# The first modulation group moves to steps 1 and 3 of the local attention, and ScalarE gets a one-column exponential behind the barrier

## The chip, the cores and the metric

The kernel is one program on 1 NeuronCore of a Trainium2 chip. The metric is device time in microseconds (us), the median of several executions. Engines are named as in the profile: PE (TensorE matmul), PEld (its weight load), DVE (VectorE), ACT (ScalarE), POOL (GpSimd), SP (SyncE, which here only issues transfers).

## What is computed

One inference step of a transformer with DEPTH = 2 layers over 640 tokens (128 of context, 512 latent: five tiles of 128), width 1024, all in float32. What matters here is that each layer has six modulation vectors per kind of token, and three groups of attention heads:

```python
def modulate(cvec, w_mod_l, b_mod_l):
    m = jnp.einsum('bd,de->be', jax.nn.silu(cvec), w_mod_l) + b_mod_l
    return jnp.split(m[:, None, :], N_MOD, axis=-1)     # sh1, sc1, g1, sh2, sc2, g2, each 1024 wide

sh1, sc1, g1, sh2, sc2, g2 = modulate(c, w_mod_l, b_mod_l)
h = rmsnorm(x, norm1_l) * (1 + sc1) + sh1
...   # projections; latent attention (A), window attention (B), 2-D neighbourhood attention (C)
x = x + g1 * (heads_out @ w_out_l)
h2 = rmsnorm(x, norm2_l) * (1 + sc2) + sh2
...   # mixture of experts on h2, added with g2
```

`w_mod` is 1024 x 6144 per layer (24 MB), so the modulation is a large read of weights for very few rows of output (one for latent, one for context tokens).

## The kernel before, in words

Each engine runs its own instruction list in program order, and the lists are tied by semaphores. A layer has four stages: entry and input projection (1), local attention, heads B and C (2), the projections of heads A (3), and their attention with the output projection (4); then the experts. All engines but SP meet at a barrier (`meet`) between stages 1, 2, 3 and 4.

The modulation of a layer is done in three groups of 2048 columns (`mod_group(L, g, ks)`): g = 0 is needed at the layer's entry, g = 1 and 2 (rows g1 to g2) later. A group is eight k slices of 128 input channels, each four matmuls of 512 columns that lie in four column strips of PE; the kernel does it in halves of four slices. Group 1 and 2 of the layer and group 0 of the next layer are done during stage 2, spread into the steps of its attention pipeline. Their weights lie in the four buffers `slot[0..3]` of `ring`, which in stage 1 hold the input projection's weights. SP (`mod_load`, line 1002) issues the load of group 1 in eight transfers of 1 MB: as soon as the last projection has left slots 0 and 1, half 0 of slots 0 and 1, then half 1 of both; once it has left slots 2 and 3, half 0 of slot 2, half 0 of slot 3, half 1 of slot 2, half 1 of slot 3. `mod_in[0]` counts half 0 of all four slots, `mod_in[1]` half 1. SP reloads half 0 with group 2 when `mod_half` tells that half 0 has been used, and half 1 when the group is finished.

Stage 2 is a software pipeline over 20 pairs of heads and tiles, in 24 steps. In step s, PE does (in this order) `turn(s-3, 0)` (transpose the normalised probabilities), `scores(s)`, `turn(s-3, 1)`, `values(s-4)` and whatever of the modulation is put there; DVE does `maximum(s)` (line 1820, both halves), `normalise(s-1)`, and for the modulation `mod_rows` (adds the bias, line 1665) and `mod_columns2`; ACT does the copies of the transposes and `exps(s)`. `scores(s)` can start once DVE's `maximum(s-1)` has released both score banks. `values` start at step 4. Where the pipeline is still filling, PE is given matmuls of zeros (`spin`, line 507) into PSUM bank 7, the bank that the modulation also uses: four each in steps 0 and 1, and three in step 3. The modulation groups stand at steps `MOD_AT = (3, 10, 17)` and the step behind each.

In ACT's list the first exponential of stage 2 is preceded by a load of its function table.

Of the kernel before, what the change touches and what calls it, by code (L numbers as in the profile page):

```python
# [29 lines left out]
ACT = mybir.ActivationFunctionType  # L30
# [5 lines left out]
DEPTH = 2  # L36
# [34 lines left out]
WHOLE = [[], [2, 4]]  # L71
ORDER = [4, 0, 1, 2, 3]
AT = [ORDER.index(t) for t in range(TILES)]
MOD_AT = (3, 10, 17)

CHUNKS = [(0, 416), (416, 384), (800, 512), (1312, 384)]
C_CQ, C_CKV, C_KPE, C_QS, C_KS, C_QN, C_KN = 0, 256, 384, 416, 672, 800, 1056
# [61 lines left out]
def program(nc, t_in, t_out):  # L139
    with ExitStack() as ctx:  # L140
        def sb(name, shape, dt=F32):
            return ctx.enter_context(nc.sbuf_tensor(name, shape, dt))
# [31 lines left out]
        cst, at = {}, 0  # L174
# [6 lines left out]
        mhalf = sb("mhalf", [P, 8])  # L181
# [149 lines left out]
        stat = {n: sb("st_" + n, [P, 8]) for n in ("mx", "m2", "nm", "sm", "es", "ri")}  # L331
# [3 lines left out]
        def two(b, n=1024):  # L335
            return ps[:, b:b + 2, :].rearrange("p a b -> p (a b)")[:, 0:n]
# [133 lines left out]
        def queries(pr, h):  # L470
            if pr["kind"] == "mla":
                return qT[0:QK, pr["heads"][h], pr["t"] * P:(pr["t"] + 1) * P]
            q = qs if pr["kind"] == "swa" else qn
            return q[64 * h:64 * h + 64, pr["c"], pr["t"] * P:(pr["t"] + 1) * P]

        def keys(pr, h, lo, hi):
            if pr["kind"] == "mla":
                return kT[0:QK, pr["heads"][h], lo:hi]
            if pr["kind"] == "swa":
                return ksT[64 * h:64 * h + 64, lo:hi]  # L480
            return knT[64 * h:64 * h + 64, pr["c"], lo:hi]

        def value_rows(pr, h, j):
            if pr["kind"] == "mla":
                return v_mla[:, j, pr["heads"][h] * 64:pr["heads"][h] * 64 + 64]
            at = 64 * h if pr["kind"] == "swa" else 128 + 64 * pr["heads"][h]
            return v_loc[:, j, at:at + 64]
# [4 lines left out]
        def split(phase, n):  # L492

            return (n, 0) if n == 1 or phase == 2 else (3, n - 3)
# [5 lines left out]
        def _(pe):  # L500
            def transpose(out, in_):
                return pe.transpose(out, in_, ident)  # L502

            def spin(b, n):

                for _ in range(n):
                    pe.matmul(ps[:, b, 0:256], zeros[:, 0:P], zeros[:, :], start=True, stop=True)
# [45 lines left out]
            def attention(L, phase):  # L553
                pairs = PAIRS[phase]
                base = PPL * L + PBASE[phase]

                def scores(p, halves):
                    pr = pairs[p]
                    for h in halves:
                        S[h].take(pe, ("s", L, phase, p))  # L560
                    for n, (at, lo, hi) in enumerate(pr["k"]):
                        for h in halves:
                            mm = pe.matmul(two(2 * h)[:, at:at + hi - lo], queries(pr, h), keys(pr, h, lo, hi),  # L563
                                           start=(at % 512 == 0), stop=True, skip_group_check=True)
                            if n == len(pr["k"]) - 1:
                                mm.then_inc(S[h].full, 1)

                def turn(p, h):
                    n = pairs[p]["n"]
                    a, d = split(phase, n)  # L570
                    T.take(pe, ("p", L, phase, p, h), frees=2 if d else 1)
                    pe.wait_ge(pn_done, base + 2 * p + h + 1)
                    for j in range(n):
                        o = two(4)[:, j * P:(j + 1) * P] if j < a else ps[:, 5, (j - a) * P:(j - a + 1) * P]
                        mm = transpose(o, pb[phase][:, p % DEEP, h, j * P:(j + 1) * P])
                    mm.then_inc(T.full, 1)

                def values(p):
                    pr = pairs[p]
                    O.take(pe, ("o", L, phase, p))  # L580
                    pe.wait_ge(T.free, T.freed[("p", L, phase, p, 1)])
                    for j in range(pr["n"]):
                        for h in range(2):
                            mm = pe.matmul(ps[64 * h:64 * h + 64, 6, 0:P], value_rows(pr, h, pr["v"][j]),  # L584
                                           pt[phase][p % 2][h][:, j * P:(j + 1) * P],
                                           start=(j == 0), stop=(j == pr["n"] - 1))
                    mm.then_inc(O.full, 1)

                for s in range(STEPS[phase]):
                    turning = 3 <= s < len(pairs) + 3  # L590
                    if phase == 4:
                        ranks(L, s - 1)
                    if phase == 2:
                        if turning:
                            turn(s - 3, 0)
                        if s == 3:
                            spin(7, 3)
                        if s < len(pairs):
                            scores(s, (0, 1))
                        if s < 2:  # L600
                            spin(7, 4)
                        if turning:
                            turn(s - 3, 1)
                        if s == len(pairs) + 1:
                            for h in range(2):
                                pe.wait_ge(S[h].free, S[h].freed[("s", L, 2, len(pairs) - 1)])
                        if s > len(pairs):
                            spin(3, 1)
                    else:
                        for h in range(2):  # L610
                            if s < len(pairs):
                                scores(s, (h,))
                                if s == 0:
                                    spin(7, 2)
                            if turning:
                                turn(s - 3, h)
                    if 4 <= s < len(pairs) + 4:
                        values(s - 4)
                    if phase == 2:
                        for g, at in enumerate(MOD_AT):  # L620
                            if s in (at, at + 1) and (g < 2 or L < DEPTH - 1):
                                ks = range(4 * (s - at), 4 * (s - at) + 4)
                                mod_group(L + g // 2, (g + 1) % 3, ks)
                        for g in (1, 2):
                            if s == MOD_AT[g - 1] + 3:
                                mod_columns2(L, g)
                        if s == MOD_AT[2] + 3 and L < DEPTH - 1:
                            mod_columns(L + 1)
                    if phase == 4:
                        if s == 1:  # L630
                            shift_logits(L)
                        beside(L, s)
# [113 lines left out]
            for L in range(DEPTH):  # L746
# [98 lines left out]


                attention(L, 4)
                E0 = NE * L

# [349 lines left out]
        def _(act):  # L1199
# [118 lines left out]
            for L in range(DEPTH):  # L1318
# [50 lines left out]
                    act.wait_ge(x7_out[TILES - 1], 16 * L)  # L1369
                meet(act, "act")  # L1370

                attention(L, 2)
                meet(act, "act")

# [283 lines left out]
        def _(dve):  # L1658
# [140 lines left out]
            def attention(L, phase):  # L1799
# [46 lines left out]
                for s in range(STEPS[phase] + 1):  # L1846
                    turning = 3 <= s < len(pairs) + 3
                    if phase == 4 and s == 2:
                        shift_logits(L)
                    if phase == 4 and s >= 1:  # L1850
                        ranked(L, s - 1)
                    for h in range(2):
                        if s < len(pairs):
                            maximum(s, h)
                        if turning and phase == 4:
                            copy(s - 3, h)
                    if phase == 4 and s >= 1:
                        projected(L, s - 1)
                    if 1 <= s <= len(pairs):
                        normalise(s - 1)  # L1860
                    if phase == 4 and s >= 1:
                        beside(L, s - 1)
                    if phase == 2:
                        for g, at in enumerate(MOD_AT):
                            if s == at + 2 and (g < 2 or L < DEPTH - 1):
                                mod_rows(L + g // 2, (g + 1) % 3)
                        for g in (1, 2):
                            if s == MOD_AT[g - 1] + 4:
                                mod_columns2(L, g)
                        if s == MOD_AT[2] + 4 and L < DEPTH - 1:  # L1870
                            mod_columns(L + 1)

            def projected(L, s):
# [140 lines left out]
            for L in range(DEPTH):  # L2014
# [19 lines left out]
                for s in range(TILES + 1):  # L2034
# [25 lines left out]
                    if s >= 1:  # L2060
                        for i in ([5, 0] if s == 1 else [s - 1]):
# [6 lines left out]
                            ks = ps[:, 5, 256:384] if i < 5 else ps[:, 5, 0:P]  # L2068
# [297 lines left out]
```

## Time and profile before

| | |
|---|---|
| median of 3 runs | 1338.06 us (1335.75 to 1340.5) |
| the profiled execution's own time | 1338.34 us |
| its span, first to last instruction | 1336.3 us |
| mean granted TensorE clock | 0.991 of full speed |
| PE busy | 1279.6 us, 96% of the span |
| DVE, ACT, POOL busy | 613.7, 358.8, 152.5 us |
| mean DMA rate | 234 GB/s |

Busy time of PE is modelled from pipelined matmuls, so 96% does not mean that it works at its peak. A stretch is read from the timeline of one engine: start, duration, and in brackets how long the engine sat idle before it and what released it. A float32 matmul stands as two records. A transfer has the time of its issue, and its landing counted from there.

### The profile page before, as it was taken

Reading aid. Unit: us, or ns where it says so; the run is one execution under the profiler, and the core shown is the slowest. Engines: PE = TensorE matmul, PEld = TensorE weight load, DVE = VectorE, ACT = ScalarE, POOL = GpSimd, SP = SyncE. Lnnn points to the kernel's source line nnn. Section 1 sums busy time; section 2 is a strip of 40 time slices with the busy share of each in tenths; the row PEclk is TensorE's granted clock in tenths of the full one; section 3 lists DMA queues with packets and bytes.
Section 4 is the critical chain, followed back from the end, with each engine's and each line's share of the span. In section 5 each row is a group of like instructions: output and inputs, shape, how many; then the busy total and the mean of one; then the engine's idle time right before and its main releaser. Section 6 shows DMA issues by size and latency. Waiting matters only on the chain. (4 is left out here: it accounts for less than half of the span.)

```text
span 1336.3 us, 17216 instructions
## 1 busy us (share of the span) xinstructions
PE 1279.6 (96%) x6042; PEld 735.3 (55%) x6042; DVE 613.7 (46%) x1519; ACT 358.8 (27%) x931; POOL 152.5 (11%) x257
## 2 busy tenths in 40 slices
PE   6999999999999999999999999989999999999997
PEld 3555555565666564444455555566666656444443
DVE  0132266444566463433343224655556536344438
ACT  1121255434343210000012114563444311100001
POOL 2210220000000110000142003000000011000014
PEclk9999999998999999999999999999899999999999
DMA  9976996499111489999694038430201139999966
GB/s 355 363 248 220 347 332 254 162 359 327 42 64 64 168 333 398 361 374 367 260 334 161 16 140 291 151 128 15 88 33 64 63 130 352 404 368 360 362 270 246
DMA packets 125441, 313.16 MB, mean 234 GB/s; under 512 B 9882, under 2 KB 58426, under 8 KB 112688
## 3 DMA queue, kind: packets, MB, share of 16 engines
q1 hardware_dynamic: 90896, 243.13, 49.8%
q0 software_dynamic: 12848, 45.39, 9.0%
q10 hardware_dynamic: 21616, 23.60, 5.3%
q8 instruction: 46, 0.75, 0.2%
q14 instruction: 35, 0.29, 0.1%
HBM read 232.14 MB, written 80.71 MB: 234 GB/s over the span
## 5 line engine op out<-in xcount | busy, mean ns | idle before, releaser
L790 PE MATMUL ps<-ring,big 128*128 128x384 f32 (+2 forms) x640 | 230.7, 520 | 1.7 <-DVE big L1773 1.3
L790 PEld LDWEIGHTS ps<-ring,big 128*128 128x128 f32 x640 | 120.3, 190 | 104.6 <-issue 63.7
L871 PE MATMUL ps<-ring,arena 128*128 128x512 f32 x384 | 169.3, 594 | 1.9 <-ACT arena L1406 1.9
L502 PEld LDWEIGHTS ps<-consts,arena 128*128 128x128 f32 (+2 forms) x880 | 103.7, 143 | 79.1 <-issue 50.9
L502 PE MATMUL ps<-consts,arena 128*128 128x128 f32 (+2 forms) x880 | 129.7, 278 | 15.7 <-ACT arena L1227 6.6
L711 PE MATMUL ps<-ring,big 128*128 128x512 f32 x320 | 143.0, 598 | 0.8
L563 PE MATMUL ps<-arena 64*128 64x128 f32 (+5 forms) x576 | 137.9, 430 | 6.1 <-DVEq L1822 3.4
L1227 ACT ACTIVATE arena<-ps 128x384 f32<-128x384 f32 (+3 forms) x140 | 69.1, 493 | 221.3 <-PE ps L502 221.3
L871 PEld LDWEIGHTS ps<-ring,arena 128*128 128x128 f32 x384 | 71.2, 190 | 83.1 <-issue 83.1
L563 PEld LDWEIGHTS ps<-arena 64*128 64x128 f32 (+1 forms) x576 | 79.4, 196 | 65.8 <-issue 57.8
L711 PEld LDWEIGHTS ps<-ring,big 128*128 128x128 f32 x320 | 59.0, 190 | 70.4 <-issue 66.4
L1410 ACT ACTIVATE arena<-ps 128x256 f32<-128x256 f32 x32 | 12.3, 385 | 300.6 <-PE ps L871 300.6
L1809 DVE TENSOR_REDUCE st_nm<-ps 128x1 f32<-128x640 f32 (+1 forms) x80 | 57.2, 717 | 75.2 <-PE ps L563 74.8
L584 PE MATMUL ps<-arena 128*64 128x128 f32 x1104 | 85.9, 280 | 1.2 <-DVEq L1963 1.2
L2122 DVE TENSOR_TENSOR arena<-arena,ps 128x256 f32<-128x256 f32 x32 | 13.5, 421 | 154.4 <-ACT arena L1410 154.4
L584 PEld LDWEIGHTS ps<-arena 128*64 128x64 f32 x1104 | 66.4, 137 | 11.9 <-issue 9.6
L2140 DVE TENSOR_TENSOR arena<-ps,arena 128x512 f32<-128x512 f32 x64 | 44.2, 691 | 55.1 <-PE ps L892 55.1
L1218 ACT ACTIVATE ring<-ps,st_nm 128x640 f32<-128x640 f32 (+1 forms) x80 | 56.4, 705 | 20.6 <-DVE st_nm L1809 20.2
L892 PE MATMUL ps<-ring,arena 128*128 128x512 f32 x128 | 57.8, 594 | 1.0 <-DVE arena L2128 1.0
L892 PE MATMUL ps<-arena 128*128 128x512 f32 x128 | 57.8, 594 | 1.0 <-DVE arena L2128 1.0
L1215 ACT ACTIVATE arena<-arena,st_nm 128x640 f32<-128x640 f32 (+4 forms) x80 | 54.0, 676 | 14.8 <-DVEq L1823 14.4
L871 PE MATMUL ps<-arena 128*128 128x512 f32 x128 | 56.3, 592 | 0.0
(237 smaller groups left out, 1481.9 us busy)
## 6 DMA issues: line engine op xcount, KB each, us to landing
ring<-in_w_mod SPq DMA_DIRECT2D x40, 1024.0 KB, 11.8
ring<-in_w_up SPq DMA_DIRECT2D x22, 1024.0 KB, 9.7
ring<-in_w_gate SPq DMA_DIRECT2D x22, 1024.0 KB, 7.6
slots<-zeros ACTq DMA_DIRECT2D x8, 2560.0 KB, 14.4
slots<-zeros SPq DMA_DIRECT2D x8, 2560.0 KB, 20.2
arena<-in_w_down SPq DMA_DIRECT2D x16, 1024.0 KB, 12.7
arena<-slots SPq DMA_DIRECT2D x30, 512.0 KB, 6.4
slots<-arena POOLq DMA_DIRECT2D x30, 512.0 KB, 9.6
```

What stands on the lines that cost most here:

```text
L502: return pe.transpose(out, in_, ident)
L563: mm = pe.matmul(two(2 * h)[:, at:at + hi - lo], queries(pr, h), keys(pr, h, lo, hi), start=(at % 512 == 0), stop=True, skip_group_check=True)
L584: mm = pe.matmul(ps[64 * h:64 * h + 64, 6, 0:P], value_rows(pr, h, pr["v"][j]), pt[phase][p % 2][h][:, j * P:(j + 1) * P], start=(j == 0), ...
L711: mm = pe.matmul(ps[:, b, :], hoT[:, i, k, :], slot[2 + half][:, k, :], start=(k == 0), stop=(k == KD - 1))
L790: mm = pe.matmul(ps[:, c, 0:CHUNKS[c][1]], hT[:, s, k, :], slot[c][:, k, 0:CHUNKS[c][1]], start=(k == 0), stop=(k == KD - 1))
L871: mm = pe.matmul(ps[:, b, :], xgT[:, b, k * P:(k + 1) * P], w_gu[q][:, :, k, :], start=(k == 0), stop=(k == KD - 1))
L892: mm = pe.matmul(ps[:, 2 + n, :], hidT[:, b, k * P:(k + 1) * P], w_dn[q][:, k, n * 512:(n + 1) * 512], start=(k == 0), stop=(k == 1))
L1215: act.activation(buf[:, 0:w], buf[:, 0:w], ACT.Exp, bias=stat["nm"][:, col], scale=-1.0, accum_out=stat["sm"][:, col]).then_inc(ex_done, 1)
L1218: act.activation(buf[:, 0:w], two(2 * h, w), ACT.Exp, bias=stat["nm"][:, col], scale=1.0, accum_out=stat["sm"][:, col]).then_inc(S[h].free, 1)
L1227: act.activation(pt[phase][p % 2][h][:, 0:a * P], two(4, a * P), ACT.Copy).then_inc(T.free, 1)
L1809: dve.tensor_reduce(nm, src, AX.X, ALU.max, negate=True).then_inc(nmax_done, 1)
L2140: return TT(yb[:, b, n * 512:(n + 1) * 512], ps[:, 2 + n, :], rowG[:, n * 512:(n + 1) * 512], ALU.mult)
```

## The change

The modulation group 1 of each layer has its half 0 at the end of step 1 and its half 1 at the end of step 3 (before: steps 3 and 4). The spins of steps 1 and 3 go; that of step 0 stays. DVE's `mod_rows` and both `mod_columns2` of this group come one step earlier. Groups 2 and 0 stay in steps 10, 11 and 17, 18. In ACT's list a one-column exponential stands between the barrier and the attention of stage 2; its result is written to a statistics buffer that stage 2 does not use.

```diff
-MOD_AT = (3, 10, 17)
+MOD_AT = ((1, 3), (10, 11), (17, 18))
...
                         if turning:
                             turn(s - 3, 0)
-                        if s == 3:
-                            spin(7, 3)
                         if s < len(pairs):
                             scores(s, (0, 1))
-                        if s < 2:
+                        if s == 0:
                             spin(7, 4)
...
                         for g, at in enumerate(MOD_AT):
-                            if s in (at, at + 1) and (g < 2 or L < DEPTH - 1):
-                                ks = range(4 * (s - at), 4 * (s - at) + 4)
+                            if s in at and (g < 2 or L < DEPTH - 1):
+                                ks = range(4 * at.index(s), 4 * at.index(s) + 4)
                                 mod_group(L + g // 2, (g + 1) % 3, ks)
                         for g in (1, 2):
-                            if s == MOD_AT[g - 1] + 3:
+                            if s == MOD_AT[g - 1][1] + 2:
                                 mod_columns2(L, g)
...
                 meet(act, "act")
+                act.activation(stat["es"][:, 0:1], mhalf[:, 0:1], ACT.Exp)
                 attention(L, 2)
...
                         for g, at in enumerate(MOD_AT):
-                            if s == at + 2 and (g < 2 or L < DEPTH - 1):
+                            if s == at[1] + 1 and (g < 2 or L < DEPTH - 1):
                                 mod_rows(L + g // 2, (g + 1) % 3)
                         for g in (1, 2):
-                            if s == MOD_AT[g - 1] + 4:
+                            if s == MOD_AT[g - 1][1] + 3:
                                 mod_columns2(L, g)
```

## Rows read from the trace of the kernel before

**Rows 1.** The page: busy time of PE.

```profile
PE 1279.6 (96%) x6042; PEld 735.3 (55%) x6042; DVE 613.7 (46%) x1519; ACT 358.8 (27%) x931; POOL 152.5 (11%) x257
```

**Rows 2.** Timeline of PE, layer 0, stage 2, steps 1 to 5.

```profile
165.05 1.99 PE L507 MATMUL ps<-zeros 128*128 128x256 f32 x8
167.16 1.14 PE L563 MATMUL ps<-arena 64*128 64x384 f32 x8
...
168.61 1.46 PE L507 MATMUL ps<-zeros 128*128 128x256 f32 x6
170.34 0.92 PE L563 MATMUL ps<-arena 64*128 64x256 f32 x8 [0.26 <-DVEq L1822]
...
172.04 3.64 PE L520 MATMUL ps<-ring,sc 128*32 128x512 f32 x32
175.61 0.66 PE L502 MATMUL ps<-consts,arena 128*128 128x128 f32 x4
...
178.44 3.64 PE L520 MATMUL ps<-ring,sc 128*32 128x512 f32 x32
182.01 0.66 PE L502 MATMUL ps<-consts,arena 128*128 128x128 f32 x4
```

**Rows 3.** Timeline of PE, layer 1, the same steps.

```profile
813.96 1.99 PE L507 MATMUL ps<-zeros 128*128 128x256 f32 x8
816.04 1.14 PE L563 MATMUL ps<-arena 64*128 64x384 f32 x8
...
820.89 3.64 PE L520 MATMUL ps<-ring,sc 128*32 128x512 f32 x32
...
830.87 0.66 PE L502 MATMUL ps<-consts,arena 128*128 128x128 f32 x4
```

**Rows 4.** Single loads of line 1002: issue duration (ns), start, then time to landing.

```profile
L1002 SPq DMA_DIRECT2D ring<-in_w_mod x1: 509/509/509, 157.1 to 157.1; - x1
...
DMA to landing us min/median/max: 12.6/12.6/12.6
...
L1002 SPq DMA_DIRECT2D ring<-in_w_mod x1: 509/509/509, 805.6 to 805.6; - x1
...
DMA to landing us min/median/max: 8.9/8.9/8.9
...
L1002 SPq DMA_DIRECT2D ring<-in_w_mod x1: 995/995/995, 806.7 to 806.7; - x1
DMA to landing us min/median/max: 15.4/15.4/15.4
```

**Rows 5.** Timeline of ACT, layer 0, the first exponentials of stage 2.

```profile
163.10 1.28 ACT L1215 ACT_TABLE_LOAD   x1 [2.59 <-DVEq L1823]
...
166.10 0.73 ACT L1215 ACTIVATE arena<-arena,st_nm 128x513 f32<-128x513 f32 x1 [0.41 <-DVEq L1823]
```

**Rows 6.** Timeline of DVE, layer 1, `maximum` of steps 4 to 6 and `mod_rows`.

```profile
826.01 0.62 DVE L1820 CUSTOM_DVE_ANT_0 arena<-ps,consts,sink 128x384 f32<-128x384 f32 x1 [1.92 <-PE ps L563]
...
832.62 0.75 DVE L1820 CUSTOM_DVE_ANT_0 arena<-ps,consts,sink 128x512 f32<-128x512 f32 x1 [3.07 <-PE ps L563]
...
835.61 0.68 DVE L1665 TENSOR_TENSOR mrow<-ps,mrow 128x512 f32<-128x512 f32 x1
836.55 0.75 DVE L1820 CUSTOM_DVE_ANT_0 arena<-ps,consts,sink 128x512 f32<-128x512 f32 x1 [0.26 <-DVE mrow L1665]
```

**Rows 7.** Stretches: length, busy time by engine, PEclk, DMA share, GB/s.

```profile
140.00:166.00 26.00, 25.34 (x103) 15.68 (x102) 7.26 (x22) 6.69 (x21) 5.98 (x14) 1.00 1.04 364
...
295.20:298.60 3.40, 3.40 (x30) 3.40 (x30) 0.65 (x4) 0.54 (x4) 0.00 (x0) 0.92 1.04 342
...
302.00:312.20 10.20, 10.20 (x27) 5.24 (x27) 3.47 (x9) 4.14 (x14) 0.00 (x0) 0.52 1.04 345
...
940.30:947.10 6.80, 6.44 (x18) 3.81 (x19) 2.62 (x11) 3.08 (x13) 0.00 (x0) 0.54 0.55 221
```

**Rows 8.** Groups of PE by line, from 294.6 to 298.5 us.

```profile
L549 PE MATMUL ps<-wr,modc 128*128 128x24 f32 x32 | 3.8, 270 | 0.0
```

**Rows 9.** Timeline of PE, start of the kernel.

```profile
9.29 3.64 PE L520 MATMUL ps<-arena,sc 128*32 128x512 f32 x16 [9.29 <-DMA arena<-in_w_mod]
12.87 3.79 PE L507 MATMUL ps<-zeros 128*128 128x256 f32 x12
16.58 1.92 PE L520 MATMUL ps<-arena,sc 128*32 128x512 f32 x16
18.43 2.86 PE L507 MATMUL ps<-zeros 128*128 128x256 f32 x12
```

More of the change, by code:

```diff
@@ L620, in attention @@
                         for g, at in enumerate(MOD_AT):
-                            if s in (at, at + 1) and (g < 2 or L < DEPTH - 1):
-                                ks = range(4 * (s - at), 4 * (s - at) + 4)
+                            if s in at and (g < 2 or L < DEPTH - 1):
+                                ks = range(4 * at.index(s), 4 * at.index(s) + 4)
                                 mod_group(L + g // 2, (g + 1) % 3, ks)
                         for g in (1, 2):
-                            if s == MOD_AT[g - 1] + 3:
+                            if s == MOD_AT[g - 1][1] + 2:
                                 mod_columns2(L, g)
-                        if s == MOD_AT[2] + 3 and L < DEPTH - 1:
+                        if s == MOD_AT[2][1] + 2 and L < DEPTH - 1:
                             mod_columns(L + 1)
@@ L1864, in attention @@
                         for g, at in enumerate(MOD_AT):
-                            if s == at + 2 and (g < 2 or L < DEPTH - 1):
+                            if s == at[1] + 1 and (g < 2 or L < DEPTH - 1):
                                 mod_rows(L + g // 2, (g + 1) % 3)
                         for g in (1, 2):
-                            if s == MOD_AT[g - 1] + 4:
+                            if s == MOD_AT[g - 1][1] + 3:
                                 mod_columns2(L, g)
-                        if s == MOD_AT[2] + 4 and L < DEPTH - 1:
+                        if s == MOD_AT[2][1] + 3 and L < DEPTH - 1:
                             mod_columns(L + 1)
```

## The prediction

> **What bounds the kernel now.** The page comes first: PE is busy 96% of the span [rows 1], so a change pays only where it shortens PE's list or a stretch in which PE waits or spins. Then I read PE's timeline in the steps that the diff touches, once for each layer [rows 2, 3]. In layer 0, step 1 ends with eight spin records at 165.05, `scores(2)` start at 167.16, `scores(3)` at 170.34, half 0 of the modulation at 172.04, step 4 at 175.61, half 1 at 178.44 and step 5 at 182.01 [rows 2]: 16.96 us from the start of the spins of step 1 to step 5. Layer 1 has the same rhythm, 813.96 to 830.87, 16.91 us [rows 3]. The reader should see two things. PE waits in front of `scores(3)` for DVE (0.26 us, behind the spin of step 3 [rows 2]): the pipeline is filling, and one score step costs 3.18 us because DVE's `maximum` must release the banks first, whatever PE does in between. And the two halves, 3.57 us each to the next instruction, stand beside spins that compute nothing. The third view is that of the loads, because the moved half needs its weights some 7 us earlier. The fourth is the granted clock.
>
> **Part by part.** *The spin of step 3* goes for nothing: it lies inside the wait for DVE [rows 2], so removing it gains 0. Its cover is DVE's `maximum(2)`, and its cost, were DVE not there, would be its 1.46 us.
>
> *The spin of step 1* is replaced by half 0. The two intervals around it are 2.11 us (165.05 to 167.16) in layer 0 and 2.08 us in layer 1. In its place stands the wait for `mod_in[0]`, if there is one, and 3.57 us.
>
> *The wait.* `mod_in[0]` is full when half 0 of slot 3 has landed. That is the second load of the later batch: issued 157.1 in layer 0 and 12.6 us on its way, so landed at 169.7; in layer 1 issued 805.6, 8.9 us, landed at 814.5 [rows 4]. PE arrives at 165.05 in layer 0 (after the last score record of step 1 is issued) and at 813.96 in layer 1. So PE waits 4.7 us in layer 0 and 0.6 us in layer 1. The difference between the layers is the DMA queues: from 140 to 166 us they are busy all the time (share 1.04, 364 GB/s [rows 7]), so the eight 1 MB loads come one behind the other. Behind the waiting instruction on PE stands `scores(2)`, and for that DVE and then ACT wait; SP's reload of half 0 comes when `mod_half` is raised, 169.7 + 3.57 = 173.3 instead of 175.6, which nothing needs before step 10.
>
> *The rest of the fill.* From `scores(2)` to `scores(3)` 3.18 us, from there to the half behind it 1.70 us, 3.57 us for it, then step 4 without a half, 175.61 to 178.44, 2.83 us [rows 2]. Step 4's own half (3.57 us) is gone. Half 1 is in time: layer 0 wants it at 178.2, and before, it ran at 178.44 with no wait; layer 1 wants it at 823.0, and its last load lands at 806.7 + 15.4 = 822.1 [rows 4].
>
> | us | layer 0 | layer 1 |
> |---|---|---|
> | wait for half 0 | 4.7 | 0.6 |
> | half 0 | 3.57 | 3.57 |
> | `scores(2)` to `scores(3)` | 3.18 | 3.15 |
> | to half 1 | 1.70 | 1.70 |
> | half 1 | 3.57 | 3.57 |
> | step 4 | 2.83 | 2.83 |
> | sum | 19.55 | 15.42 |
> | before | 16.96 | 16.91 |
> | difference | +2.6 | -1.5 |
>
> (For layer 1 the score step and the 1.70 come from the 4.85 us between 816.04 and 820.89, step 4 from the 9.98 us between 820.89 and 830.87 less two halves [rows 3].)
>
> *Does it survive step 5?* Steps 5 to 9 have no modulation and DVE is nearly full there, so DVE's own chain must be checked. Before, DVE idled 3.07 us ahead of `maximum(5)` under half 1 [rows 6]; that idle time is gone. In layer 1 `maximum(4)` starts 1.54 us into step 4 (826.01 against a step start of 820.89 + 3.58 = 824.47), so at 826.55 + 1.54 = 828.1; by the 3.93 us from `maximum(5)` to `maximum(6)` with `mod_rows` in between [rows 6], `maximum(5)` starts at 832.0 (before 832.62), and `maximum(6)`, without `mod_rows` (0.68 + 0.26), at 835.0 (before 836.55): 1.5 us gained there too. POOL's and ACT's share in this can take or give some 0.9 us per layer (the 0.6 us gain at `maximum(5)` against 1.5): I keep that as a bound.
>
> *DVE's additions* only move one step ahead; they keep their distance to the half.
>
> *The exponential.* It brings the table load (1.28 us [rows 5]) in front of the wait for the first `maximum`, in which ACT idles 2.59 us. Before, ACT had caught up by the second pair: it idled 0.41 us ahead of it, waiting for DVE [rows 5]. No instruction of PE before step 3 needs an exponential. So it gains 0; if this cover were gone, 1.28 us per layer, 2.6 in all, is the upper bound, and one small instruction of ACT in an idle stretch is the lower one, 0. The Trainium skill (ScalarE: Activation LUTs, What ACT_TABLE_LOAD costs) puts a switch at about 1.28 us plus 1.38 us of drain, 2.66 us; by that the upper bound would be 5.3 us for both layers. The trace agrees with the 1283 ns alone and shows no idle stretch of that size behind it.
>
> **The clock.** Rows show TensorE at its lower level (1.2 GHz) twice behind a warm stretch: PEclk 0.52 over 302.0 to 312.2 and 0.54 over 940.3 to 947.1 [rows 7]. What PE did before the first: 3.8 us of matmuls with 24 columns each [rows 8], busy by the record, but little streamed. After the change PE streams nothing for 4.7 us in layer 0, less than it did there. So I expect the clock to fall in or just behind that wait. The price from both sides: 0 if it holds; at the lower level the 16 records of a half-size group took 3.64 us against 1.92, and 12 spins 3.79 against 2.86, together 2.65 us more over the first 7 us of dense work [rows 9]; a low stretch as long as those of rows 7 would reach half 1 as well and cost up to 5. Half 0 alone at 1.2 GHz costs 3.6 at most, half of it if the clock returns while it runs, 1.8. I take 2.2, between 1.8 and 2.65, since the dense half follows at once. The Trainium skill (TensorE: Matmul & The Clock Gate, Why this matters for your kernels) warns of PE-idle gaps between bursts for the same reason. That the trace agrees with it in full no row shows, since no warm stretch before has so long a wait.
>
> **Sum.** +2.6 - 1.5 + 2.2 = +3.3 us on the profiled execution's 1338.34, of which the span is 1336.3 and 2.0 us lie around it. The median of the runs, 1338.06, is 0.3 lower; on it, 1341.3 us.
>
> **The rivals.**
> *A. The wait, and the clock falls* (forecast, 0.50): 1341.3, own range 1339.8 to 1344.
> *B. The wait, the clock holds* (0.27). For: every step around it is dense, and one low stretch behind a weak one is not a rule. Against: rows 7 and 8. 1338.06 + 1.1 = 1339.2.
> *C. Faster: the weights are there* (0.13). The loads land before PE arrives in both layers. Decisive is a landing of slot 3's half 0 at 166 or earlier in layer 0, 3.7 us earlier than the row. Then each layer gains 16.9 less 14.85, 2.1 us: 1338.06 - 4.2 = 1333.9; with part of it, 1336. Against: the queues are full [rows 7], and none of the earlier issues is moved.
> *D. Low for longer, or in both layers* (0.10): the spins also kept PE streaming in steps 1 and 3, and without them the clock falls in both layers or stays low over half 1: 1338.06 + 1.1 + 5 = 1344.2 and above.
>
> **Range and chances.** B, A and the lower half of D are inside, C's partial gain too: 1336.0 to 1344.8 leaves out about 0.08 below and 0.08 above; without C, A and B alone are 1338.5 to 1344. A measurement of this kernel tells about 0.3%, 4.0 us, from no change: 1334.0 and 1342.1 are the bounds. Faster: half of C, 0.06. Slower: D and some 0.4 of A, 0.30. Within: 0.64.
>
> **What would show it.** Right: in layer 0 an idle stretch of PE of 4 to 5 us ahead of line 520, released by a DMA, `scores(2)` near 173.3, and PEclk under 1 between 168 and 178; in layer 1 a wait under 1 us, `scores(2)` near 818.1 and step 5 near 1.5 us earlier relative to the start of stage 2; ACT_TABLE_LOAD right behind the barrier with `exps(1)` at its old distance to `maximum(1)`. Wrong: no DMA release ahead of line 520, or ACT ahead of its old place with PE following it, or step 10 no later in layer 0 although `scores(2)` is (then another engine paces the steps in between).

## The result and the profile after

| us | before | after |
|---|---|---|
| median | 1338.35 (1334.87 to 1342.05, 13 runs) | 1343.4 (1340.38 to 1347.93, 13 runs) |
| profiled execution, its span | 1338.34, 1336.3 | 1347.93, 1345.9 |

The ratio after to before is 1.0046, 95% interval 1.0031 to 1.0061: some 6 us slower (4 to 8); the medians lie 5.05 us apart. The profiled execution after is the slowest of its 13, so its span (+9.6) overstates the change. What can be compared to a tenth of a microsecond is the length of stage 2, from the first score matmul to the first projection matmul of stage 3. The timeline of PE gives both ends; first the kernel before:

```profile
161.21 0.49 PE L563 MATMUL ps<-arena 64*128 64x256 f32 x2 [0.23 <-PEq L424]
261.13 0.67 PE L815 MATMUL ps<-wuq,arena 128*128 128x512 f32 x1 [0.23 <-POOLq L424]
...
809.77 0.49 PE L563 MATMUL ps<-arena 64*128 64x256 f32 x2 [0.23 <-PEq L424]
902.23 0.67 PE L815 MATMUL ps<-wuq,arena 128*128 128x512 f32 x1 [0.23 <-POOLq L424]
```

and the changed kernel:

```profile
161.38 0.49 PE L563 MATMUL ps<-arena 64*128 64x256 f32 x2 [0.23 <-PEq L424]
266.99 0.67 PE L813 MATMUL ps<-wuq,arena 128*128 128x512 f32 x1 [0.39 <-POOLq L424]
...
816.33 0.49 PE L563 MATMUL ps<-arena 64*128 64x256 f32 x2 [0.23 <-PEq L424]
909.92 0.67 PE L813 MATMUL ps<-wuq,arena 128*128 128x512 f32 x1 [0.23 <-POOLq L424]
```

Stage 2 took 99.9 and 92.5 us and takes 105.6 and 93.6: +5.7 in layer 0, +1.1 in layer 1. These 6.8 us lie within the ratio's 4 to 8. The rest of the 9.6 us lies between the two stages 2 and behind the second, and varies as much among the kernels below (546 to 549 us between them, 434 to 440 behind).

The fill of layer 0, timeline of PE (answers to [rows 2]):

```profile
164.15 1.14 PE L563 MATMUL ps<-arena 64*128 64x384 f32 x8
170.08 5.64 PE L520 MATMUL ps<-ring,sc 128*32 128x512 f32 x32 [4.79 <-DMA ring<-in_w_mod]
175.65 1.14 PE L563 MATMUL ps<-arena 64*128 64x384 f32 x8
...
178.83 0.92 PE L563 MATMUL ps<-arena 64*128 64x256 f32 x8 [1.56 <-DVEq L1821]
...
180.53 3.64 PE L520 MATMUL ps<-ring,sc 128*32 128x512 f32 x32
184.10 0.65 PE L502 MATMUL ps<-consts,arena 128*128 128x128 f32 x4
...
186.94 0.66 PE L502 MATMUL ps<-consts,arena 128*128 128x128 f32 x4
```

The reader should see the wait of 4.79 us that a DMA ended, and behind it a half that takes 5.64 us instead of 3.64. The load it waited for, single, with its time to landing (answers to [rows 4]):

```profile
L1000 SPq DMA_DIRECT2D ring<-in_w_mod x1: 508/508/508, 157.2 to 157.2; - x1
...
DMA to landing us min/median/max: 12.7/12.7/12.7
```

157.2 + 12.7 = 169.9, and PE starts at 170.08. The changed kernel in layer 1 (answers to [rows 3]):

```profile
821.29 3.64 PE L520 MATMUL ps<-ring,sc 128*32 128x512 f32 x32 [0.69 <-DMA ring<-in_w_mod]
824.86 1.14 PE L563 MATMUL ps<-arena 64*128 64x384 f32 x8
...
829.89 5.13 PE L520 MATMUL ps<-ring,sc 128*32 128x512 f32 x32
834.95 0.66 PE L502 MATMUL ps<-consts,arena 128*128 128x128 f32 x4
...
837.78 0.65 PE L502 MATMUL ps<-consts,arena 128*128 128x128 f32 x4
```

Here the wait is 0.69 us, and it is half 1, in step 3, that is slow, 5.13 us. The DMA queues of the changed kernel show what differs between the layers. From 140 to 166 us all engines are busy (share 1.04), and over 140 to 170 us a second queue takes 38.6% of them:

```profile
q1 hardware_dynamic: 3405, 6.78, 60.3%
q10 hardware_dynamic: 3568, 3.62, 38.6%
```

ACT issued two fills of `slots` with zeros, 2560 KB each, at 134.1 and 134.6; the second landed 19.9 us later, 10 us after the first load of the modulation had been issued. Over 796 to 826 us, in layer 1, this queue moves nothing. That the wait of layer 0 would be as short as that of layer 1 without these fills was not tried.

Stretches of the changed kernel (length, busy time by engine, PEclk, DMA share, GB/s; answers to [rows 7]):

```profile
162.00:168.00 6.00, 3.29 (x22) 2.23 (x18) 3.37 (x10) 3.19 (x10) 6.00 (x12) 0.95 1.05 391
168.00:174.60 6.60, 4.52 (x24) 1.26 (x28) 0.56 (x2) 0.13 (x2) 0.01 (x1) 0.53 0.98 359
174.80:180.00 5.20, 3.39 (x31) 1.77 (x22) 2.62 (x8) 2.00 (x5) 0.18 (x1) 1.00 0.55 182
...
830.20:833.40 3.20, 3.20 (x20) 0.71 (x16) 2.60 (x5) 1.48 (x5) 2.19 (x2) 0.57 1.00 341
833.60:840.00 6.40, 6.21 (x59) 3.77 (x52) 2.88 (x8) 3.15 (x8) 2.81 (x4) 1.00 1.04 386
```

The granted clock averages 0.53 over 168 to 174.6 in layer 0 and 0.57 over 830.2 to 833.4 in layer 1, which is the lower level (1.2 GHz) for most of either stretch. In the kernel before it was full throughout stage 2, here over the whole of it in each layer:

```profile
161.20:261.10 99.90, 92.15 (x812) 55.88 (x812) 54.98 (x184) 54.73 (x141) 13.26 (x26) 1.00 0.69 250
809.80:902.20 92.40, 84.75 (x744) 53.67 (x744) 53.66 (x180) 54.73 (x141) 13.46 (x26) 1.00 0.50 178
```

ACT's list (answers to [rows 5]) has the table load right behind the barrier, and the second pair's exponential stands where it stood, now with 1.43 us of idle time before it instead of 0.41:

```profile
160.78 1.28 ACT L1370 ACT_TABLE_LOAD   x1
162.07 0.20 ACT L1370 ACTIVATE st_es<-mhalf 128x1 f32<-128x1 f32 x1
...
166.27 0.72 ACT L1213 ACTIVATE arena<-arena,st_nm 128x513 f32<-128x513 f32 x1 [1.43 <-DVEq L1822]
```

### The profile page after: what moved, and what is told of

Same layout as the page of the kernel before. It is cut to its first block and busy times, and to the rows that moved or that the text cites. A ratio compares the mean times of both kernels' runs of the same rounds, so it can differ in the third digit from the quotient of the medians.

```text
span 1345.9 us, 17162 instructions
## 1 busy us (share of the span) xinstructions
PE 1277.8 (95%) x6014; PEld 731.1 (54%) x6014; DVE 614.0 (46%) x1519; ACT 359.2 (27%) x933; POOL 152.0 (11%) x257
```

## The experiments

Theory W is the prediction's: the wait for the weights in layer 0 and the clock behind it make the loss. Theory S: the removed spins let the clock fall by themselves. X: the exponential has a price. All lengths are those of stage 2 in one profiled execution; ratios are against the kernel before on the same chip, with their 95% interval.

| kernel | ratio | layer 0 | layer 1 |
|---|---|---|---|
| before | | 99.9 | 92.5 |
| changed | 1.0046 (1.0031 to 1.0061) | 105.6 | 93.6 |
| e1 exponential alone | 1.0006 (0.9987 to 1.0026) | 99.9 | 92.4 |
| e2 changed, spins in both gaps | 1.0023 (1.0008 to 1.0038) | 103.4 | 91.8 |
| e3 half 0 loaded first | 1.0098 (1.0079 to 1.0117) | 107.2 | 97.9 |
| e4 steps 2 and 3 | 0.9994 (0.9982 to 1.0007) | 100.9 | 91.2 |
| e5 new place in layer 0 alone | 1.0046 (1.0028 to 1.0065) | 105.8 | 92.6 |
| e6 new place in layer 1 alone | 0.9993 (0.9976 to 1.0011) | 99.9 | 93.6 |
| e7 before without the spins | 1.0029 (1.0009 to 1.0048) | 102.6 | 96.1 |
| e8 layer 0 as before, layer 1 in 2 and 3 | 0.9997 (0.9980 to 1.0013) | 99.9 | 91.3 |
| e9 e2 with POOL's additions early | 1.0039 (1.0022 to 1.0055) | 102.7 | 93.1 |
| e10 e8 with POOL's additions early | 1.0076 (1.0053 to 1.0099) | 105.2 | 94.2 |
| e11 changed, spins in step 1 alone | 1.0019 (1.0003 to 1.0035) | 105.0 | 91.9 |
| e12 changed, spins in step 3 alone | 1.0040 (1.0023 to 1.0057) | 105.6 | 91.4 |

**e1, the exponential alone.**

```diff
                 meet(act, "act")
+                act.activation(stat["es"][:, 0:1], mhalf[:, 0:1], ACT.Exp)
                 attention(L, 2)
```

> The kernel before with the one-column exponential alone. Theory W (PE's wait for the weights of half 0 in layer 0, and the clock that falls behind it, make the loss) and theory S (the removed spins let the clock fall, wait or no wait): no difference, the table load stands earlier in ACT's list and nothing else moves, 1338.4 us. Theory X (the exponential has a price or a gain of its own): up to 2.6 us less, or as much of the 5 us loss as is its own.

1337.64 us against 1337.73. The interval alone would leave room for 2 us either way, but stage 2 is as long as before in both layers. X falls.

**e2, spins back under the wait and in step 3.**

```diff
+                        if s == 3:
+                            spin(6, 3)
                         if s < len(pairs):
                             scores(s, (0, 1))
                         if s == 0:
                             spin(7, 4)
+                        if s == 1:
+                            spin(7, 9 if L == 0 else 1)
```

> The changed kernel with spins put back where they can't cost time: nine in layer 0 and one in layer 1 in front of half 0, inside the wait for its weights, and three in step 3 into the bank of the values, which is free there. W and S both say that the clock holds through the fill: the half in layer 0 takes 3.6 us instead of 5.6, that in layer 1 3.6 instead of 5.1, so some 3.5 us less than the changed kernel, about 1340 us; the wait of 4.8 us in layer 0 stays, now under spins, so it is still 1 to 2 us slower than before. If the clock is not part of the cause, it stays at 1343.4.

1341.24 us. By the ratios half of the loss is gone, though their intervals overlap; the stages show it more sharply. Timeline of PE in layer 0 of e2:

```profile
164.73 4.15 PE L507 MATMUL ps<-zeros 128*128 128x256 f32 x18
169.53 3.64 PE L520 MATMUL ps<-ring,sc 128*32 128x512 f32 x32 [0.65 <-DMA ring<-in_w_mod]
...
184.38 0.66 PE L502 MATMUL ps<-consts,arena 128*128 128x128 f32 x4
```

The weights come no earlier, but the half takes 3.64 us again. The granted clock is 1.00 throughout stage 2, and the stage is 2.2 us shorter than in the changed kernel in layer 0 and 1.8 in layer 1: that is the clock's part. Without it, layer 0 is still 3.5 us longer than before, and layer 1 0.7 shorter (+3.49 and -0.64 by the timeline).

**e3, half 0 of all four slots first.**

```diff
                 for half in range(2):
                     sp.wait_ge(S[half].full, S[half][("in", L, TILES - 1)])
-                    for part in range(2):
-                        mod_load(L, 1, part, (2 * half, 2 * half + 1))
+                    mod_load(L, 1, 0, (2 * half, 2 * half + 1))
+                mod_load(L, 1, 1)
```

> The changed kernel with one edit on SP: half 0 of all four slots is loaded first, half 1 of all four behind it. W: half 0 of slot 3 lands at about 164.5 us in layer 0, so PE doesn't wait at half 0 and waits some 1.6 us at half 1 (landing about 175); in layer 1 neither waits by more than 0.5. Without a clock fall about 1337 us. S: the clock falls in spite of it, in one or both layers, and costs 1.5 to 2 each: 1339 to 1341.

In layer 0 PE did not wait at half 0 (it started at 164.78), as said, and yet the kernel is the slowest of all, 1% behind. Half 1 waits 5.57 us there and, with the clock low again, takes 6.58. In layer 1, where no wait over 0.5 us was expected, PE waits 0.77 us at half 0 and 3.83 at half 1. Half 1 of layer 0, timeline of PE:

```profile
178.87 6.58 PE L520 MATMUL ps<-ring,sc 128*32 128x512 f32 x32 [5.57 <-DMA ring<-in_w_mod]
```

A stretch of e3 shows why the landing came 4 us later than I had worked out:

```profile
155.00:158.00 3.00, 2.57 (x17) 1.74 (x15) 0.62 (x2) 1.62 (x6) 0.00 (x0) 1.00 0.45 130
```

With only two loads for slots 0 and 1 issued early, the queue runs dry until the last projection frees slots 2 and 3: 130 GB/s over 155 to 158, where the kernel before moved 406:

```profile
155.00:158.00 3.00, 2.82 (x17) 1.86 (x15) 0.57 (x2) 1.34 (x5) 0.00 (x0) 1.00 1.06 406
```

The early half 1 of slots 0 and 1 is what fills that gap. This order got half 0 in on time at the cost of half 1. Whether another order has both in time was not tried.

**e4, half 0 in step 2, the spins of step 1 kept.**

```diff
-MOD_AT = ((1, 3), (10, 11), (17, 18))
+MOD_AT = ((2, 3), (10, 11), (17, 18))
...
-                        if s == 0:
+                        if s < 2:
                             spin(7, 4)
```

> The changed kernel with half 0 in step 2 instead of step 1, and the spins of step 1 kept. W: in layer 0 PE reaches half 0 at 168.3, the weights land at 169.8, so it waits 1.5 us and not 4.8, and half 0 lies where PE waits for DVE anyway: step 5 some 0.6 us earlier than before in layer 0 and 2.1 us earlier in layer 1, less 0.6 each that the following steps take back; no clock fall: 1336.5 us. S: the missing spins of step 3 alone let the clock fall: 1338 to 1340.

1337.4 us, no difference from before. PE waited 1.60 us at half 0 and 0.49 at half 1 in layer 0, and there is no low clock in stage 2, although the spins of step 3 are missing in both layers. Locally it is +1.0 and -1.2 us.

**e5 and e6, one layer each.** `MOD_AT` becomes a list by layer, with the spins of the untouched layer kept:

```diff
-MOD_AT = ((1, 3), (10, 11), (17, 18))
+MOD_AT = [((1, 3), (10, 11), (17, 18)), ((3, 4), (10, 11), (17, 18))]    # e5; e6 the other way round
```

> The changed kernel with the new place of the halves in layer 0 alone; layer 1 has them in steps 3 and 4 with its spins, as before. W (the wait of layer 0 and the clock that falls behind it): the whole loss stays, 1342.5 to 1343.5 us, with stage 2 of layer 0 about 5.7 us longer than before and that of layer 1 unchanged. S (the removed spins cost in both layers): about half of the loss, 1340.5.

> The counterpart: halves in steps 1 and 3 in layer 1 alone, layer 0 as before. W: a wait of 0.7 us, stage 2 of layer 1 between 1 us shorter (clock holds) and 1.1 us longer (clock falls behind step 3 as in the changed kernel); 1337.4 to 1339.2 us, no difference that can be told. S: 1340.5.

By the ratios the whole loss is layer 0's (1.0046 against 1.0046), and layer 1 alone can't be told from before. By the stages layer 0 has 5.7 of the 6.8 us: stage 2 of layer 1 in e6 is 1.1 us longer as in the changed kernel, with a low clock again. The changed kernel's price is the place of half 0 in the layer where the loads are late.

**e7, the kernel before without the spins of steps 1 and 3.**

> The kernel before without the spins of steps 1 and 3, nothing else. They stand inside PE's waits for DVE, so without a clock effect nothing moves: 1338 us (W). S: the clock falls in the fill of stage 2 in one or both layers, and the half behind it takes 5 us or more instead of 3.6: 1339.5 to 1342.

```diff
-                        if s == 3:
-                            spin(7, 3)
...
-                        if s < 2:
+                        if s == 0:
                             spin(7, 4)
```

1343.55 us, 1.0029: here S was right and W, by which nothing moves, was wrong. Timeline of PE in layer 0 of e7, and behind it in layer 1:

```profile
167.85 1.14 PE L563 MATMUL ps<-arena 64*128 64x384 f32 x8 [2.04 <-DVEq L1820]
...
171.01 1.65 PE L563 MATMUL ps<-arena 64*128 64x256 f32 x8 [1.54 <-DVEq L1820]
...
173.42 5.58 PE L520 MATMUL ps<-ring,sc 128*32 128x512 f32 x32
...
818.98 2.02 PE L563 MATMUL ps<-arena 64*128 64x384 f32 x8 [2.01 <-DVEq L1820]
...
822.98 1.65 PE L563 MATMUL ps<-arena 64*128 64x256 f32 x8 [1.15 <-DVEq L1820]
```

and two stretches of it, one in each layer:

```profile
171.10:177.70 6.60, 6.60 (x35) 2.75 (x39) 4.37 (x10) 2.77 (x8) 2.37 (x2) 0.52 0.58 211
...
819.60:829.60 10.00, 8.86 (x46) 4.16 (x46) 6.31 (x16) 3.87 (x12) 2.55 (x3) 0.51 0.29 111
```

In layer 0 the scores start at the same distances as before, since PE waits there for DVE, and the clock falls in the second of the two gaps without spins, 2.0 and 1.5 us long: `scores(2)` still take 1.14 us, `scores(3)` 1.65 instead of 0.92. In layer 1 it falls behind the first gap already: `scores(2)` take 2.02 us. So one gap of 2.0 us was enough there. Stage 2 gets 2.7 and 3.6 us longer.

**e11 and e12, one cover each.** Which of the two gaps of the changed kernel does it?

> The changed kernel with spins in front of half 0 alone (nine in layer 0, one in layer 1), none in step 3. If the long wait is what lets the clock fall, layer 0 holds (stage 2 103.4 us) and layer 1, whose wait is only 0.7 us, is as in the changed kernel (93.6, a fall near step 3). If the gap of step 3 does it, both layers fall and cost 1.5 to 2 each.

> The changed kernel with the three spins of step 3 alone, none in the wait. If the wait is what lets the clock fall in layer 0, stage 2 stays at 105.6 us there; layer 1 holds (91.8), since only step 3 was weak in it. About 1342 us.

Timeline of PE in layer 0, e11 first and then e12:

```profile
178.54 4.84 PE L520 MATMUL ps<-ring,sc 128*32 128x512 f32 x32
...
169.75 5.81 PE L520 MATMUL ps<-ring,sc 128*32 128x512 f32 x32 [4.75 <-DMA ring<-in_w_mod]
```

With spins under the wait alone the clock held through half 0 in layer 0 but fell later, in step 3 (half 1 took 4.84 us; stage 2 105.0); layer 1 held, against what was expected. With spins in step 3 alone it fell during the wait in layer 0 (half 0 took 5.81 us) and held in layer 1. The ratios, 1.0019 and 1.0040, point to the cover of the wait as the more valuable one, but their intervals overlap, so this isn't settled. Both gaps can let the clock fall, and a profile of one execution does not say how often.

**e8, a version from the pieces.** Layer 0 as before, layer 1 in steps 2 and 3 (`MOD_AT` by layer, spins of step 1 in both).

> The best of the pieces so far: layer 0 as before (its weights land too late for more), layer 1 with the halves in steps 2 and 3 and the spins of step 1 kept. PE reaches half 0 in layer 1 when the weights have landed and waits 0.5 us or less at half 1; stage 2 of layer 1 some 1.5 us shorter, nothing longer in layer 0: 1336.5 us by W, with the clock holding. S: the missing spins of step 3 in layer 1 cost what is gained, 1338.

Locally as said (-1.2 us in layer 1, +0.0 in layer 0, no low clock in stage 2), 1338.5 us in all, which is no difference that can be told.

**e9 and e10, POOL's additions moved.** In both layers 0.8 to 0.9 us are lost between step 5 and step 10. POOL and DVE of the changed kernel in layer 0 (timeline):

```profile
186.40 2.23 POOL L1555 TENSOR_TENSOR arena<-arena,consts 128x960 f32<-128x960 f32 x1
...
187.70 1.47 DVE L1843 TENSOR_SCALAR arena<-arena,st_ri 128x384 f32<-128x384 f32 x2
...
190.03 0.75 DVE L1819 CUSTOM_DVE_ANT_0 arena<-ps,consts,sink 128x512 f32<-128x512 f32 x1 [0.26 <-DVE mrow L1664]
...
192.34 0.75 DVE L1843 TENSOR_SCALAR arena<-arena,st_ri 128x384 f32<-128x384 f32 x2
```

The same pair of operations takes 1.47 us in `normalise(3)` and 0.75 in `normalise(4)`; beside the former, POOL adds its last bias. Half 1 used to cover this (the 3.07 us of [rows 6]).

```diff
-                    if 2 <= p < 6:
-                        if p == 2:
+                    for head in {2: (0,), 3: (1, 2, 3)}.get(p, ()):
+                        if head == 0:
                             pool.wait_ge(rpb_in, 16 * (L + 1))
-                        bh = bias[:, p - 2, :].rearrange("p (j c) -> p j c", j=15)
+                        bh = bias[:, head, :].rearrange("p (j c) -> p j c", j=15)
```

> The changed kernel with the spins put back under the wait and in step 3, and with POOL's four additions of the 2-D bias done at pairs 2 and 3 (one and three of them) instead of one each at pairs 2 to 5. Theory P: what steps 5 to 9 take back (0.8 us per layer) is POOL's last addition, which runs beside normalise(3) and makes it 1.5 us instead of 0.75, and half 1 no longer hides that. Then stage 2 is 102.7 us in layer 0 (103.4 with the spins alone) and 91.1 in layer 1 (91.8). If the rest of DVE's chain is the cause, both stay.

> Layer 0 as before, layer 1 with the halves in steps 2 and 3, and POOL's additions at pairs 2 and 3: by P stage 2 is 99.9 us in layer 0 (there they are hidden under half 1) and 90.5 in layer 1, 1.9 us less than before in all, 1336.2 us. Without P 91.3 in layer 1.

In layer 0 of e9 P was right to the tenth: 102.7 us, with `normalise(3)` at 0.75. But layer 1 is 1.2 us longer than in e2, not 0.7 shorter, and e10 is 5.2 us longer in layer 0. The three additions in a row shut DVE out; timeline of POOL and DVE in layer 0 of e9:

```profile
165.24 6.58 POOL L1559 TENSOR_TENSOR arena<-arena,consts 128x960 f32<-128x960 f32 x3
...
166.99 5.39 DVE L1847 TENSOR_SCALAR arena<-arena,st_ri 128x384 f32<-128x384 f32 x2
```

`normalise(0)`, 1.02 us long in the kernel before, ends only 0.6 us behind POOL. In layer 0 of e9 this lies under the wait for the weights and costs nothing. In e10 it does not: PE waits 4.27 us for it, and the clock falls behind that wait as well (0.50 over 172.9 to 176.2). So P is shown in layer 0 only.

## Why the prediction was right, and where it was not

**The direction and the wait.** Right. Predicted 4.7 and 0.6 us of wait, found 4.79 and 0.69; `scores(2)` to `scores(3)` 3.18, to half 1 1.70, half 1 3.57, step 4 2.84. Step 5 of layer 0 starts 4.76 us later, counted from the start of stage 2, where the sum had 2.6 + 2.2 = 4.8. e5 and e6 put the loss that the ratios can tell into layer 0. The load that PE waited for landed at 169.9 where 169.7 was said.

**The clock in layer 0.** Right in place and size: taken at 2.2 us, by the difference of e2 to the changed kernel 2.2. In e12, whose only uncovered gap is the wait, the clock falls too. The value was a choice between 1.8 and 2.65, so the exact hit is in part luck. Rows 7 were also misread: in the kernel before the first low stretch does not start at 302.0 but at 298.1 (the granted clock is 0.50 over 298.6 to 302.0 already) and lasts 13.7 us, so "up to 5" was no upper bound. The Trainium skill warns of PE-idle gaps between matmul bursts (TensorE: Matmul & The Clock Gate, Why this matters for your kernels). The wait of 4.79 us agrees with that; e7 goes beyond it, since its gaps of 2.0 and 1.5 us are shorter than those that the page warns of, and the clock fell behind them all the same.

**The clock in layer 1.** Missed. Step 5 was to come 1.5 us earlier, counted from the start of stage 2; it comes 0.35 us later (21.45 against 21.10 us). The sum gave layer 1 -1.5 us and let it keep it; the spins were priced at nothing because they lie inside waits for DVE. That holds for the time that they take and not for what they do to the clock. The cover I named for them (DVE's `maximum(2)`) was the wrong thing to name: what went was the streaming. Rival D had this case, at 0.10; e2 puts it at 1.8 us in layer 1, and e7 shows it alone.

**"Does it survive step 5?"** The bound of 0.9 us per layer was there, the value taken was 0, and 0.8 to 0.9 came in both layers (e2: step 5 starts 2.7 us late and the stage ends 3.5 late). The 3.93 us from `maximum(5)` to `maximum(6)` was a row of a step in which POOL did not add; `normalise(3)` beside POOL is 0.7 us longer, and e9 took this back in layer 0.

**The sum.** +2.6 - 1.5 + 2.2 = 3.3 was forecast; 2.6 - 1.5 + 2.2 + 1.8 + 1.7 = 6.8 is what the rows of stage 2 give. So the mechanism was right and the size half of it: two terms, taken as zero, made up the rest. The median, 1343.4, is inside the range because the range was wide enough for both; it lies above the 1342.1 from which on the prediction called a result slower, a case that it gave 0.30. The fall in both layers, which the prediction kept for rival D, came true at a smaller price than D's: 2.2 + 1.8 = 4.0 us against 5.

**The exponential.** Right at 0 (e1).

**Rival C** had its deciding point right and its way to get there was closed: e3 made half 0 land in time, and paid at half 1.

**Open.** How often the clock falls in each of the two gaps; stage 4 has a low stretch in each layer of all kernels, of 7 to 20 us, and its length moves single spans by a few microseconds. That this is chance of the execution is not shown; it was not told apart from an effect of the change.

## What to carry to other kernels

Before work is moved up the list, work out when its data lands, in each layer apart: the same edit waited 0.7 us in one layer and 4.8 us in the other, and only in the latter did another queue hold a large part of the DMA engines. Filler matmuls inside a wait cost no time here and were worth some 2 us per layer (e2): ask of each removal what PE streams in their place. Work that stood in a wait also covers slow operations of its neighbours, and these appear when it moves.

## What the runs showed of the hardware

In e7 PE's granted clock fell to half behind short gaps, with no long idle time: in layer 0 in the second of two gaps of 2.0 and 1.5 us, in layer 1 behind the first, of 2.0 us. It does not fall each time: a gap of 1.56 us in step 3 brought it down in layer 0 of e11, and the same gap left it full in layer 1. And POOL's 128 x 960 additions keep DVE's SBUF-to-SBUF scaling out: 0.75 us beside nothing, 1.47 beside one addition, 5.39 beside three in a row. The Trainium skill (SBUF — State Buffer, Terms) says that the two engines share one pair of ports, which one instruction holds for its full time while the loser "**fully blocks**"; the trace agrees, and shows that between two additions in a row DVE does not get in either.
